# A decoder layer on one core: one conditioning part computed by rows, a norm's transposes in four banks, the last tiles' variance in fewer steps, and a causal mask moved from TensorE to VectorE

## The reference, cut to what matters

```
ada = (c @ w_ada + b_ada)                # shift_m, scale_m, gate_m, shift_f, scale_f, gate_f
h = rms_norm(x, g_pre_mix) * (1 + scale_m) + shift_m
qa, ka, va, qb, kb, vb, f_logit, gate_logit = split(h @ w_in)
o_a = sliding_window_attention(rope(qa), rope(ka), va, sinks)     # window 128
s = qb.kb / sqrt(64) + cum[t] - cum[s]                            # cum: running sum of log_sigmoid(f_logit)
o_b = softmax(where(key <= query, s, -inf)) @ vb                  # causal, 8 heads
merged = sigmoid(gate_0) * (o_a @ w_branch_a) + sigmoid(gate_1) * (o_b @ w_branch_b)
x = x + gate_m * rms_norm(merged @ w_out, g_post_mix)
h = rms_norm(x, g_pre_ffn) * (1 + scale_f) + shift_f
y = (silu(h @ w_g) * (h @ w_u)) @ w_ffn_out
x = x + gate_f * rms_norm(y, g_post_ffn)
```

## Time and profile before

| | us |
|---|---|
| median of 3 runs | 1456.67 (1455.56 to 1457.21) |
| the profiled execution's own time | 1452.32 |
| its span | 1450.6 |
| TensorE busy | 1401.9 (97%) |
| VectorE busy | 993.5 (68%) |
| ScalarE busy | 546.3 (38%) |
| GpSimd busy | 582.0 (40%) |

### The profile page before, as it was taken

The page is one execution under the profiler, slowest core; times in us unless marked ns, Lnnn a source line. Parts: engine busy times, 40 slices in busy tenths (PEclk is TensorE's granted clock), DMA queues, the critical chain, the costliest instruction groups (busy, mean ns, idle before and its releaser), DMA issues.

```text
span 1450.6 us, 19821 instructions
## 1 busy us (share of the span) xinstructions
PE 1401.9 (97%) x6923; PEld 1146.8 (79%) x6932; DVE 993.5 (68%) x1421; ACT 546.3 (38%) x1115; POOL 582.0 (40%) x467
## 2 busy tenths in 40 slices
PE   4999998999999999999999999999999999999998
PEld 2898776777777888888888788888888888888886
DVE  4876777565663666676755786667776666697768
ACT  3611467455463000101343533333333333464443
POOL 1415845233145445334302226777777764100000
PEclk9999999999999999999999999999999999999999
DMA  9500021111303644444242234444444446876763
GB/s 350 145 15 15 24 81 41 55 37 52 117 23 105 172 116 145 116 117 131 87 159 89 73 117 136 129 128 126 130 131 133 145 145 209 296 242 194 250 232 116
DMA packets 174811, 185.69 MB, mean 128 GB/s; under 512 B 15904, under 2 KB 128648, under 8 KB 174096
## 3 DMA queue, kind: packets, MB, share of 16 engines
q1 hardware_dynamic: 168336, 178.87, 39.3%
q10 hardware_dynamic: 6400, 5.83, 1.2%
HBM read 148.98 MB, written 35.69 MB: 127 GB/s over the span
## 4 chain that ended last, share of the span: by engine, by line
PE 86%; DVE 7%; issue 2%; ACT 2%; DMA 1%; POOL 1%; SPq 1%; DVEq 0%; ACTq 0%; POOLq 0%
PE PS L1944 69%; PE PS L2073 8%; PE PS L2127 2%; PE PS L2154 2%; PE PS L2181 1%; PE PS L2182 1%; DMA wada<-in_w_ada_dram 1%; ACT pt_hi L1051 1%; DVE s_row L1490 1%; PE PS L1955 1%; DVE ada_acc L1352 1%; POOL s_row L872 1%; DVE rope_b L1425 1%; DVE mx L1471 1%; DVE pt_lo L1514 1%
## 5 line engine op out<-in xcount | busy, mean ns | idle before, releaser
L918 POOL TENSOR_TENSOR ws_lo<-s_tmp,ws_hi 128x512 fp32r<-128x512 f32 x76 | 116.4, 1531 | 87.7 <-ACT ws_hi L1204 87.7
L1514 DVE TENSOR_TENSOR pt_lo<-PS,pt_hi 128x512 fp32r<-128x512 f32 (+3 forms) x128 | 74.5, 582 | 84.4 <-ACT pt_hi L1051 84.0
L1944 PE MATMUL PS<-T_hi,ws_hi 128*128 128x512 f32 x320 | 124.5, 389 | 0.0
L1944 PE MATMUL PS<-T_lo,ws_hi 128*128 128x512 f32 x320 | 124.5, 389 | 0.0
L1944 PE MATMUL PS<-T_hi,ws_lo 128*128 128x512 f32 x320 | 124.5, 389 | 0.0
L1944 PE MATMUL PS<-db_hi,da_hi 128*128 128x512 f32 x308 | 119.8, 389 | 0.0
L1944 PE MATMUL PS<-db_lo,da_hi 128*128 128x512 f32 x308 | 119.8, 389 | 0.0
L1944 PE MATMUL PS<-db_hi,da_lo 128*128 128x512 f32 x308 | 119.8, 389 | 0.0
L1944 PE MATMUL PS<-act_hi,w_hi 128*128 128x512 f32 x288 | 113.1, 393 | 0.8 <-DVE w_lo L1746 0.8
L1944 PE MATMUL PS<-act_hi,w_lo 128*128 128x512 f32 x288 | 112.2, 389 | 0.0
L1944 PE MATMUL PS<-act_lo,w_hi 128*128 128x512 f32 x288 | 112.1, 389 | 0.0
(11 more groups left out here) (318 smaller groups left out, 3718.0 us busy)
## 6 DMA issues: line engine op xcount, KB each, us to landing
dn_raw<-ff_dram SPq DMA_DIRECT2D x66, 256.0 KB, 4.3
adaraw<-in_w_ada_dram SPq DMA_DIRECT2D x32, 512.0 KB, 4.0
wraw<-in_w_in_dram SPq DMA_DIRECT2D x25, 512.0 KB
wraw<-in_w_ffn_in_dram SPq DMA_DIRECT2D x24, 512.0 KB, 5.0
ff_dram<-sl SPq DMA_DIRECT2D x22, 512.0 KB, 6.1
w2t<-in_w_ffn_out_dram SPq DMA_DIRECT2D x22, 512.0 KB, 6.8
w2sum_dram<-w2s SPq DMA_DIRECT2D x11, 1024.0 KB, 5.8
dn_raw<-w2sum_dram SPq DMA_DIRECT2D x44, 256.0 KB, 4.5
```

The lines of the kernel that those rows point to most:

```text
L918: pool.tensor_tensor(ws_hl[i][1][:, :, :], left(par, i), ws_hl[i][0][:, :, :].bitcast(F32), ALU.subtract)\
L1514: nc.vector.tensor_tensor(pt_hl[gp % 3][1][:, 0:n], PS[:, 4 + gp % 2, 0:n], pt_hl[gp % 3][0][:, 0:n].bitcast(F32), ALU.subtract).then_inc( ...
L1944: ins = nc.tensor.matmul(out_ap, lhs[a], rhs[b], start=first and i == 0, stop=last and i == 2)
```

## The change

Five edits are made together.

```diff
-    adarow = at("adarow", R0 + KB, [1, 2, NT])
+    adarow = at("adarow", R0 + KB, [1, 3, NT])
+    cs_diag = at("cs_diag", R0 + CS + 10 * KB, [P, 2, P])
+    AHEAD = 1
-    ADA_DVE = ((0, 0, 4), (2, 0, 4), (1, 0, KD), (3, 0, KD))
-    N_COLS = 2
+    ADA_DVE = ((0, 0, 4), (2, 0, 4), (1, 0, 4), (3, 0, KD))
+    N_COLS = 1
+    ROW_BANK = (6, 7, 5)
-        return g % 4 if g < 2 * KD else 2 + g % 2
+        return 2 + g % 2 if 2 * KD <= g < 3 * KD else g % 4
...
-            for i in range(2):
+            for i in range(3):
                 act.wait_ge(row_ready, i + 1)
-                nc.scalar.activation(adarow[:, i], PS[0:1, 6 + i], ACT.Copy).then_inc(row_ok, 1)
+                nc.scalar.activation(adarow[:, i], PS[0:1, ROW_BANK[i]], ACT.Copy).then_inc(row_ok, 1)
...
+            act.wait_ge(z_var, 2)
             for t in range(4, NTOK):
                 z_square(NTOK + t)
-                act.wait_ge(z_var, t - 2)
-                nc.scalar.activation(rms[:, 24 + t:25 + t], var[:, 24 + t:25 + t], ACT.Sqrt).then_inc(z_rms, 1)
+                act.wait_ge(z_sq, NTOK + t + 1)
+                nc.scalar.activation(rms[:, 24 + t:25 + t], ssq_z[:, 2 * t:2 * t + 1], ACT.Sqrt, bias=var[:, 24 + t:25 + t],
+                                     scale=1.0 / D).then_inc(z_rms, 1)
...
+                past = w - P
+                if r > A_T:
+                    dve.wait_ge(s_taken, rows_taken(r))
+                nc.vector.tensor_tensor(cs_diag[:, :, :], cs[:, :, past:w], maskb[:, :, P:2 * P], ALU.add).then_inc(dve_step, 1)
+                step[0] += 1
+                made = [step[0], step[0]]
+                for h in range(2 if past else 0):
+                    nc.vector.tensor_tensor_reduce(out=s_row[i][:, h, 0:past], in0=src[h][:, 0:past], in1=cs[:, h, 0:past],
+                                                   scale=-SM, scalar=BIG, op0=ALU.add, op1=ALU.min,
+                                                   accum_out=nm_past[:, h:h + 1]).then_inc(dve_step, 1)
+                    step[0] += 1
+                    made[h] = step[0]
                 for h in range(2):
-                    ins = nc.vector.tensor_tensor_reduce(out=s_row[i][:, h], in0=src[h][:, 0:w], in1=cs[:, h, 0:w], scale=-SM,
-                                                         scalar=BIG, op0=ALU.add, op1=ALU.min,
-                                                         accum_out=nm[:, r % 4, h:h + 1])
-                    ins.then_inc(s_taken, 1)
+                    dve.wait_ge(dve_step, made[h])
+                    nc.vector.tensor_tensor_reduce(out=s_row[i][:, h, past:w], in0=src[h][:, past:w], in1=cs_diag[:, h],
+                                                   scale=-SM, scalar=nm_past[:, h:h + 1] if past else BIG, op0=ALU.add,
+                                                   op1=ALU.min, accum_out=nm[:, r % 4, h:h + 1]).then_inc(s_taken, 1)
...
+                    for k in range(KD):
+                        h_tmp_part(KD * (2 + t) + k)
                     if t == 1:
                         dve.wait_ge(h_lo, 3 * KD)
                         for k in range(KH):
                             rebuild(k)
-                    for k in range(KD):
-                        h_tmp_part(KD * (2 + t) + k)
...
+            unit_lo(0)
             for q in range(4):
                 t_lo_part(q)
-            unit_lo(0)
...
+            nc.vector.tensor_scalar(var[:, 28:32], sq[:, 4:NTOK, 1], 1.0 / D, EPS, ALU.mult, ALU.add).then_inc(z_var, 1)
...
-            def z_rstd(t0, t1, nth):
-                cols, sq = slice(24 + t0, 24 + t1), ssq_z[:, 2 * t0:2 * t1].rearrange("p (t h) -> p t h", h=2)
-                dve.wait_ge(z_sq, NTOK + t1)
-                link(nc.vector.tensor_tensor(var[:, cols], sq[:, :, 0], sq[:, :, 1], ALU.add))
-                nc.vector.tensor_scalar(var[:, cols], var[:, cols], 1.0 / D, EPS, ALU.mult, ALU.add).then_inc(z_var, 1)
+            def z_rstd(cols, nth):
                 dve.wait_ge(z_rms, nth)
                 link(nc.vector.reciprocal(rstd[:, cols], rms[:, cols]))
...
-                elif g >= 2 * KD + 2:
+                elif g >= 3 * KD + 2:
+                    pe.wait_ge(h_tmp, g - 3)
+                elif 2 * KD + 2 <= g < 3 * KD:
                     pe.wait_ge(h_tmp, g - 1)
...
             row_columns(1)
-            ada_columns(2, False)
-            warm_up()
+            ada_row(2)
+            ada_rest(2)
+            warm_up(4)
+            row_columns(2)
             ada_columns(3, True)
-            warm_up()
+            warm_up(10)
...
-            for k in range(KD):
+            pe.wait_ge(h_hi, 1)
+            pe.wait_ge(wv_split, 1)
+            for i, (a, b) in enumerate(TERMS):
+                if a == 1:
+                    pe.wait_ge(h_lo, 1)
+                    transpose_group(4, xin[:, 0:4])
+                for t in range(2):
+                    cols = slice(t * P, (t + 1) * P)
+                    nc.tensor.matmul(PS[:, va_bank(t), 0:WV - VB_1], act_hl[a][:, 0, cols], wv_hl[b][:, 0, VB_1:WV],
+                                     start=i == 0, stop=False)
+                    nc.tensor.matmul(PS[:, 5 + t % 2, 0:VB_1], act_hl[a][:, 0, cols], wv_hl[b][:, 0, 0:VB_1],
+                                     start=i == 0, stop=False)
+            for k in range(1, KD):
...
-                for h in range(2):
-                    ins = nc.tensor.matmul(dst[h][:, w - P:w], identb[:, :], maskb[:, 0, P:2 * P], start=False, stop=True)
                 ins.then_inc(s_ready, 1)
...
-                    if j == 1 and k >= 5:
-                        pe.wait_ge(xn_ok, 3 + NTOK)
-                        transpose_group(3 * KD + k - 5, xn)
+                    if j == 1 and k >= AHEAD:
+                        if k == AHEAD:
+                            pe.wait_ge(y_taken, NTOK)
+                            pe.wait_ge(xn_ok, 3 + NTOK)
+                        transpose_group(3 * KD + k - AHEAD, xn)
                 ins.then_inc(ff_ready, 1)
-            for k in range(3, KD):
+            for k in range(KD - AHEAD, KD):
                 transpose_group(3 * KD + k, xn)
```

More of the change, by code:

```diff
@@ L107, in hybrid_layer @@
     mx = small("mx", [P, 2, 2])
+    nm_past = small("nm_past", [P, 2])
     nm = small("nm", [P, 4, 4])
@@ L1926, in _ @@
             gain("c11", 3)
-            z_rstd(0, 4, 1)
+            sq = ssq_z[:, :].rearrange("p (t h) -> p t h", h=2)
+            dve.wait_ge(z_sq, NTOK + 4)
+            link(nc.vector.tensor_tensor(var[:, 24:28], sq[:, 0:4, 0], sq[:, 0:4, 1], ALU.add))
+            nc.vector.tensor_scalar(var[:, 24:28], var[:, 24:28], 1.0 / D, EPS, ALU.mult, ALU.add).then_inc(z_var, 1)
+            nc.vector.tensor_scalar(var[:, 28:32], sq[:, 4:NTOK, 1], 1.0 / D, EPS, ALU.mult, ALU.add).then_inc(z_var, 1)
+            z_rstd(slice(24, 28), 1)
             for t in range(4):
@@ L1935, in _ @@
                 link(nc.vector.tensor_tensor(fin[:, t % 2], usum[tt][:, :], grow[:, 1, 0:NT], ALU.mult))
-                z_rstd(t, t + 1, t - 2)
+                z_rstd(slice(24 + t, 25 + t), t - 2)
                 finish(t, (usum[tt], c22[tt]), (fin[:, t % 2], c22[tt][:, :]))
@@ L1964, in ada_row @@
                 for k in range(KD // 2, KD):
-                    nc.tensor.matmul(PS[0:1, 6 + nth], pcols[:, k:k + 1], wada[:, j, k], start=(k == KD // 2), stop=False)
+                    nc.tensor.matmul(PS[0:1, ROW_BANK[nth]], pcols[:, k:k + 1], wada[:, j, k], start=(k == KD // 2), stop=False)
             def ada_rest(nth):
                 pe.wait_ge(acc_ready, nth + 1)
-                nc.tensor.matmul(PS[0:1, 6 + nth], ones[:, 0:1], ada_acc[:, nth % 2], start=False, stop=True).then_inc(row_ready, 1)
+                nc.tensor.matmul(PS[0:1, ROW_BANK[nth]], ones[:, 0:1], ada_acc[:, nth % 2], start=False, stop=True).then_inc(row_ready, 1)
             def row_columns(nth):
@@ L1984, in ada_columns, with warm_up @@
                 ins.then_inc(ada_used, 1)
-            def warm_up():
-                for n in range(8):
+            def warm_up(count):
+                for n in range(count):
                     nc.tensor.matmul(PS[:, 6, :], identb[:, :], maskb[:, :, :].rearrange("p a n -> p (a n)"), start=True, stop=True)
@@ L2126, in scores @@
                             rows = slice(h * HALF, (h + 1) * HALF)
-                            nc.tensor.matmul(dst[h][:, c0:c0 + n], qb_hl[pb % 2][x][rows, i * P:(i + 1) * P],
-                                             kb_hl[pb % 2][y][rows, c0:c0 + n], start=(e == 0),
-                                             stop=(e == 2 and c0 + n < w))
-                for h in range(2):
-                    ins = nc.tensor.matmul(dst[h][:, w - P:w], identb[:, :], maskb[:, 0, P:2 * P], start=False, stop=True)
+                            ins = nc.tensor.matmul(dst[h][:, c0:c0 + n], qb_hl[pb % 2][x][rows, i * P:(i + 1) * P],
+                                                   kb_hl[pb % 2][y][rows, c0:c0 + n], start=(e == 0), stop=(e == 2))
```

(1 more changed line is left out.)

## The result

The changed kernel takes 1465.89 us (median of 4 runs, 1464.24 to 1466.86) against 1456.12 for the kernel before beside it; the ratio is 1.0079, 95% interval 1.0063 to 1.0094. It is slower by about 10 us, where no change was forecast, and outside the range. The profiled execution took 1466.86 us with a span of 1465.1, against 1452.32 and 1450.6. The kernel before scatters by some 5 us itself: beside the experiments its median was 1452.94, 1454.67 and 1452.85 us (29, 27 and 25 runs), so the loss may be 1 to 3 us larger than the 10 of this pair.

What follows compares the result with a forecast made beforehand. TensorE was taken as the bound, busy 1401.9 of 1450.6 us. Start -2.0, norm -3.0, end -1.3 and mask +6.3 sum to 0.0, laid on the runs' median: 1456.7 us; own range 1454 to 1459.5, overall 1451.5 to 1461.

Steps and rivals of the forecast that it cites:

- mask part: Second branch: moving the mask from TensorE to VectorE costs +6.3 us, bounds +1 to +11.
- Now head 0 comes last but one: Widest row: VectorE frees head 0 for ScalarE's exponential 2.65 us after starting the row, formerly 1.2, at 326.33.
- That is +1.43: Widest row: exponential and everything up to the transposes at 330.00 come 1.43 us later; 5.7 over four head pairs.
- The score rounds: Rows 4 to 7: each round waiting for VectorE grows 0.35 us, delaying the scores of row 7 by 0.86.
- rows 0 to 3: Outside head pair 0, VectorE's added work there is covered; TensorE's 0.06 us for 12 rows brings in 0.7.
- Slow rival: Mask: each added VectorE instruction costs its whole duration, 0.72 us a row; total +3.1, 1459.8 us; chance 0.20.
- threshold of 0.70 a row: Mask: the price in us per row from which the slower case decides, where the total passes +2.9.
- Start: Start up to the first products: columns ready 1.8 us earlier and TensorE at 2.4 GHz; -2.0 us, bounds -1.4 and -2.7.
- rival 3: Start gives nothing: clock stays low, or VectorE, contending with GpSimd, bounds the k tile stage; total +2.0, 1458.7; chance 0.07.
- Norm: Second norm to feed-forward products: transposes interleaved with matmuls, next weights' low part earlier; -3.0 us, bounds -2.3 and -3.5.
- the tie of the prediction: Second norm: the second token half's products need GpSimd's last group at 820.9 us, while GpSimd ends at 821.0.
- End: Last four token tiles: root starts 0.4 us earlier per tile and the last round is shorter; -1.3 us, bounds -1.1 and -1.5.

Runs made afterwards that it cites:

- mask_only: The kernel before with the mask edit alone (causal mask added on VectorE instead of TensorE); ratio to the kernel before 1.0101.
- no_mask: The changed kernel with the mask left on TensorE; start, second norm and end as changed; ratio to the kernel before 0.9978.
- head_order: The changed kernel, but VectorE finishes head 0, past then diagonal block, before starting head 1; ratio to the kernel before 1.0071.
- add_early: The changed kernel with the mask's addition moved ahead of VectorE's wait for the scores in rows 1 to 7; ratio to the kernel before 1.0023.
- no_add: The changed kernel with the block split but without the addition, so the second branch's mask is left out; ratio to the kernel before 1.0009.
- late_head0: The kernel before with one number changed: waiters for head 0 in the second branch wait until head 1 is read too; ratio 1.0033.
- no_pe_mask: The kernel before without TensorE's 64 mask matmuls and nothing in their place; ratio to the kernel before 0.9996.

## Why the prediction was wrong

**The clause that failed** is in the mask part: "Now head 0 comes last but one", which gives "That is +1.43", and from this, it says, everything to the transposes at 330.00 follows. The lateness was read right in kind and followed down one road, ScalarE's, while a second waiter stood at the same semaphore: the projection whose product goes into head 0's bank. A head pair costs 2.65, not 1.43:

- The score rounds: +1.0 up to the widest row's scores, against 0.86 forecast for that row's round. A row costs 0.61 where nothing disturbs it (the 768 wide row: 1.76 before from its start to the last accumulator, 2.37 now), against 0.57. That step was right where GpSimd is quiet; in the two widest rows it is 0.74 and 0.91, and 0.80 in row 2, whose addition meets a GpSimd instruction too.
- The widest row's head 0: ScalarE gets it 3.11 after the row's start instead of 2.65, since the addition took 0.65 from start to start and not 0.34. TensorE stops there: +1.6. This is the missed wait. The transposes that the prediction watched then find their row ready (no idle time before 341.14). How much of the stop is the missed wait's alone can be read from mask_only: there VectorE's normalised row is ready at 335.06, 5.20 later than before (328.11 + 1.75), and the transposes start at 335.87, 5.87 later (rows below). Along the road that the prediction followed TensorE would have been 0.67 earlier, so the missed wait is worth about 0.7 a pair in the first three pairs, 2.0 in all (an estimate); the rest of the pair's error is the larger price of the rows.
- Another +0.25 in rows 0 to 3 cancels -0.25 behind the wait. They were taken as covered, with -0.7 for TensorE.

The rows of VectorE's normalising and of TensorE's transposes, first in the kernel before, then in mask_only; the transposes at 330.00 are in the earlier trace rows:

```profile
328.11 1.75 DVE L1508 TENSOR_SCALAR s_row<-s_row,rden 128x1024 f32<-128x1024 f32 x2
...
333.64 1.42 DVE L1522 TENSOR_SCALAR s_row<-s_row,rden 128x1024 f32<-128x1024 f32 x2
...
335.87 0.60 PE L2165 MATMUL PS<-ident,s_row 128*128 128x128 f32 x4
```

**Sum of the branch.** Forecast 4 x 1.43 + 1.3 - 0.7 = 6.3. Measured 4 x 2.65, the prelude (the rows before head pair 0's transposes) 1.9, and 1.4 in the last pair: 13.9. The 1.4 are VectorE's normalisings, 3.93 instead of 2.45 us, the second of which ran into GpSimd's subtraction. The prediction had no term for it. In the prelude the largest wait was not the 0.99 that the prediction looked at, which stayed, but one for VectorE's low part of the first branch's probabilities (253.25: 1.51 us, before 0.15). The bounds of 1 and 11 did not hold it. The row's price of 0.57 was near in most rows; what it does to each waiter, and what VectorE's later work then meets on GpSimd, was the error.

**Slow rival.** It named the mechanism (VectorE's addition meets GpSimd's) and it is in the trace in 11 of 32 additions (8 meet GpSimd's normalising, 3 its split of the weights), but its total of +3.1 falls short as well, since it shared the missed wait. Its threshold of 0.70 a row did not decide.

**Start.** -0.2 in the trace, against -2.0; 0.9999 timed alone. The columns were done at 38.63 instead of 39.69, although the loads came 0.6 later in this execution: a gain of 1.65, forecast 1.8. What failed is the next clause, that VectorE is 1.8 earlier "k tile by k tile": in the changed kernel one scaling took 1.90 beside GpSimd (43.13) instead of 0.48, and by the fourth k tile TensorE waited for the low parts. In no_mask and head_order that scaling took 0.48 with the same code, and the start gained 1.9, so part of the miss is the run's chance. The bound by VectorE was rival 3's second half, given 0.07. Its first half, the clock, did not happen: 1.00 where 0.50 had been. That "the window 38 to 43 us has a granted clock of 0.50" would hold for the kernel before in general was a reading of one execution.

**Norm.** -2.4 against -3.0, inside its bounds. The second half's products waited 0.64 for GpSimd's last low part, the tie of the prediction, and the next weights came in at 846.82, again 0.69 late.

**End.** -1.2 against -1.3. The root starts 0.04 after the accumulator's read instead of 0.48, and the first operation on the last product 0.10 after that product's end (1458.74 + 0.39 to 1459.23).

The condition set for being wrong, "a head pair no longer than before", did not occur; the longer pair was foreseen, its size was not.

## What to carry to other kernels

When an edit delays the release of a buffer, list every wait on that semaphore, on every engine, and price each: here ScalarE's was priced and TensorE's was not. An operation put between a product and its reader is paid in each round of a loop whose two sides wait for each other, even when both engines look half idle; ahead of the wait the same addition cost less than a quarter (2.0 of 8.8 us). Where two engines hold each other up, a shift of 1 us can change which of their instructions meet: look at what the shifted instruction will run beside. And one profiled execution has one pattern of clock and of such meetings: take the price of a part from two traces, or from one in which the stretch is at the full clock.

## What the runs showed of the hardware

**A VectorE operation on two SBUF operands queues behind a running GpSimd instruction.** Of the two GpSimd instructions that begin at 330.57 the first ends at 331.48; the addition starts at 331.03 and ends at 331.75, 0.27 behind it. The row before, in the same timeline:

```profile
325.83 0.81 POOL L876 TENSOR_SCALAR s_row<-s_row,rden 128x640 f32<-128x640 f32 x1
326.37 0.55 DVE L1498 TENSOR_TENSOR cs_diag<-cs,maskb 128x256 f32<-128x256 f32 x1 [1.41 <-PE PS L2162]
```

GpSimd ends at 326.64 and the addition at 326.92, 0.28 behind. All 11 long additions fit this, and where GpSimd began 0.1 us after the addition (additions at 307.87 and 365.17) it kept its 0.42 to 0.43. One addition (245.97) kept its 0.43 although a GpSimd instruction had begun 0.04 us before it, so who begins first is not told exactly by these rows. The Trainium skill ("SBUF — State Buffer", the section on the two separate sides) says that VectorE and GpSimd hold a shared pair of ports exclusively for a whole instruction, and that an operation with two SBUF inputs is among those that need it. These rows agree; the custom instructions, which read PSUM and SBUF, kept their 1.08 beside the same GpSimd work.

**A VectorE operation with one SBUF operand does so too.** VectorE's second normalising of the last head pair (half of L1526, 1024 columns) takes 0.73 alone. In all fourteen traces it ended 0.55 or 0.56 behind the GpSimd instruction that ran at its start: it took 1.52 in the eight where this was the cast to `oa_hi`, and 2.83 to 2.87 in the six where it was the subtraction to `oa_lo` (2.7 long). These six are the changed kernel, mask_only, add_early, no_add, late_head0 and no_pe_mask. Neither operation was edited in any of them; only their timing had moved.

**A stretch at 1.2 GHz stood behind short pauses of TensorE, and not in each run.** The same pause of 0.9 us near 197 us was followed by 3.4 us at 0.50 in the changed kernel and by full clock in mask_only:

```profile
197.90:201.30 3.40, 3.40 (x30) 2.60 (x28) 1.62 (x6) 2.15 (x8) 0.51 (x2) 1.00 0.00 0
```

Each such stretch cost 1.0 to 1.6 us where TensorE was the bound, and nothing in head_order, where it fell before a pause. Which run gets one was not settled, and neither was whether the pause is its cause; no experiment varied it by itself.
